# Stick-breaking attention: the second sigmoid is written over the scores in PSUM, and the scan reads it there

## The chip, the cores and the metric

One core of a Trainium2 chip runs the whole kernel in one launch. The metric is the device time in microseconds (us) of one execution, as the median of the runs made; every time below is in us or, for single instructions where it says so, in ns. The engines are PE (TensorE, matrix products and transposes), DVE (VectorE), ACT (ScalarE), POOL (GpSimd) and SP (SyncE, which here only issues transfers). PSUM is the memory into which PE writes, in eight banks of 512 fp32 values per partition; SBUF is the working memory.

## What is computed

The kernel is one inference step of a two-layer trunk: an attention layer with a compressed key-value latent, then a stick-breaking attention layer, each followed by a squared-ReLU network. The change touches the prompt part of the stick-breaking attention alone (1024 frames, 16 heads of 64):

```python
def sb_attend(q, q_pos, k, v, k_pos):
    z = jnp.einsum('bqhd,bkhd->bhqk', q, k, preferred_element_type=jnp.float32) * (SB_HEAD_DIM ** -0.5)
    mask = (k_pos[None, :] < q_pos[:, None])[None, None]
    log_keep = jnp.where(mask, jax.nn.log_sigmoid(-z), 0.0)
    suffix = lax.cumsum(log_keep, axis=3, reverse=True) - log_keep
    a = jnp.where(mask, jnp.exp(jax.nn.log_sigmoid(z) + suffix), 0.0)
    return jnp.einsum('bhqk,bkhd->bqhd', a.astype(v.dtype), v)
```

In products instead of logarithms: the weight of key k is sigmoid(z_k) times the product of sigmoid(-z_j) over all later keys j. The running product over the keys, from the last to the first, is a scan.

## The kernel before

`sb_attention_stage` handles two heads at a time, a pair; eight pairs make the stage. A pair is 16 steps. Step n is one head `a` and one block of 128 queries `q`, and has (q+1)*128 keys, its width `used`: 128 to 1024. The steps of a pair have, in order, the blocks q = 0, 1, 0, 1, 2, 3, 2, 3, 4, 5, 4, 5, 6, 7, 6, 7. Loops run over two pairs a body, `Fori` for three bodies and then a last one written out. The text counts the steps of a pair from 0 to 15.

One step passes through the engines like this:

- PE, `scores(i, n)` (L2015, L2019): q times the high and the low part of the keys into score buffer n % 2, and the causal mask added by one small product. A score buffer is two banks; there are two of them, banks 0 to 3.
- ACT, `weights(i, n)`: `keep` = sigmoid(-z) (L1850, tile e_u, two buffers in SBUF), then `take` = sigmoid(z) (L1854, tile e_b, four buffers in SBUF). Both read the scores in PSUM.
- DVE, `scan(i, n)` (L1956): the running product of `keep` from the last key to the first, into `rest` (e_r). Its second data operand is one zero per partition in SBUF, read for every element.
- POOL, `weigh(i, n)` (L1927): `take` times `rest`, in place in `take`; both in SBUF.
- PE, `transposes(i, n, last)` (L2040, for the next pair's queries and keys L2026): blocks of 128 keys, up to four to a task, into one of three task banks (4 to 6).
- ACT, `transposed_hi` (L1876; L1858 for queries and keys), copies a task bank rounded to the high part, and DVE, `transposed_lo` (L1980, L1962), writes the difference between the task bank and the high part.
- PE, `values(i, unit, last)` (L74 to L76), after every second step: weights times values into bank 7.

Each engine works its list in the order written out. In the body for n the lists are: PE scores(n+5), transposes(n+1), and for odd n values; ACT weights(n+5), transposed_hi(n+2); DVE scan(n+3), transposed_lo(n); POOL weigh(n+3). Semaphores tie the lists together. Those that matter here are `kept` (counts L1850), `taken` (L1854), `scanned` (L1956), `weighted` (L1927) and `t_lo`: scores(n) waits until take(n-2) is done, since both use one score buffer; keep(n) waits for scan(n-2), since both use one `keep` buffer; scan(n) waits for keep(n) and for weigh(n-2); the transposes of a task wait for the `lo` of three tasks earlier; scores of step 0 of a pair wait for its queries and keys.

Of the kernel before, what the change touches and what calls it, by code (L numbers as in the profile page):

```python
# [33 lines left out]
ACT = mybir.ActivationFunctionType  # L34
# [3 lines left out]
P = 128  # L38
D_MODEL = 1024
KT = D_MODEL // P  # L40
SEQ = 1024
# [1694 lines left out]
def sb_attention_stage(nc, io, scratch, raw):  # L1736
# [7 lines left out]
    with nc.cleanup_on_exit(), ExitStack() as ctx:  # L1744
        def sb(name, shape, dt=F32):
            return ctx.enter_context(nc.sbuf_tensor(name, shape, dt))
# [7 lines left out]
        v = [[sb(f"e_v{u}{s}", [P, NPT, 3 * SB_DIM], F32R) for s in "hl"] for u in range(2)]  # L1754
        raw_heads(nc, ctx, "e")
        v_raw = raw[2][:, :, :, 0, :]
        keep = [sb(f"e_u{u}", [P, SEQ]) for u in range(2)]
        take = [sb(f"e_b{u}", [P, SEQ]) for u in range(4)]
        rest = [sb(f"e_r{u}", [P, SEQ + 1]) for u in range(2)]
        pt = [[sb(f"e_pt{u}{s}", [P, NPT, GQ], F32R) for s in "hl"] for u in range(2)]  # L1760
# [6 lines left out]
        v_in, v_hi, v_lo = (signal(f"e_v_{x}") for x in ("in", "hi", "lo"))  # L1767
        arrived = [*raw_in, v_in]
        s_done = signal("e_s")
        kept, taken = signal("e_kept", 2), signal("e_taken", 2)  # L1770
        scanned, weighted = signal("e_scan", 2), signal("e_weighted", 2)
        t_done, t_hi, t_lo = signal("e_t"), signal("e_t_hi"), signal("e_t_lo", 3)
        pv_done, o_done = signal("e_pv", 2), signal("e_o", 1)
# [63 lines left out]

        @block.scalar
        def _(act):
            kept.start(act)  # L1840
            taken.start(act)
            o_done.start(act)

            def weights(i, n, last=False):

                first, _, used = score_columns(S.where(n)[2])
                z = score[n % 2][:, first:first + used]
                s_done.wait(act, S.STEPS * i + n + 1)
                scanned.wait(act, S.STEPS * i + n - 1)
                act.activation(keep[n % 2][:, 0:used], z, ACT.Sigmoid, scale=-SB_SCALE).then_inc(kept.sem, 1)  # L1850
                if n >= 4:

                    t_done.wait(act, S.PREPARE + TASKS * i + S.before(n - 3, last))
                act.activation(take[n % 4][:, 0:used], z, ACT.Sigmoid, scale=SB_SCALE).then_inc(taken.sem, 1)  # L1854

            def prepare_hi(pair, index, m):
                hi = operand(pair, index)[0]
                act.copy(hi, task_bank(m)[:, 0:hi.shape[1]]).then_inc(t_hi.sem, 1)  # L1858

            def values_hi(p, pair):  # L1860
                v_in.wait(act, 16 * (p + 1))
                pv_done.wait(act, S.UNITS // 2 * (p - 1))
                act.copy(v[pair][0][:].rearrange("p t (b c) -> p t b c", b=3)[:, :, ::2, :],
                         v_raw).then_inc(v_hi.sem, 1)

            def transposed_hi(i, n, last):
                unit, at = n // 2, (n % 2) * P
                for j, (kind, task) in enumerate(S.tasks(n, last)):
                    m = S.before(n, last) + j
                    t_done.wait(act, S.PREPARE + TASKS * i + m + 1)  # L1870
                    if kind == "prepare":
                        prepare_hi(1 - S.where(n)[0], task, m)
                        continue
                    pv_done.wait(act, S.UNITS * i + unit - 1)
                    s0 = task[0][1]
                    act.copy(pt[unit % 2][0][:, s0:s0 + len(task), at:at + P],  # L1876
                             task_bank(m)[:, 0:len(task) * P].rearrange("p (s c) -> p s c", c=P)).then_inc(
                                 t_hi.sem, 1)

            def output(i, g):  # L1880
                pv_done.wait(act, S.UNITS * i + 2 * g + 2)
                o_out[g % 2].wait(act, 16 * (S.GROUPS // 2 * i + g // 2))
                act.copy(o_st[g % 2][:], bank[:, 7, 0:GQ]).then_inc(o_done.sem, 1)

            def step(i, n, last):

                if not (last and n + S.AHEAD >= S.STEPS):
                    weights(i, n + S.AHEAD, last)
                pair, m = S.where(n)[0], n % S.PAIR_STEPS
                if m == S.VALUES_AT and not (last and pair == 1):  # L1890
                    values_hi(2 * i + pair + 1, 1 - pair)

            def body(i, last):
                for n in range(S.STEPS):
                    m = n + S.OUTPUT_LAG
                    if not (last and m >= S.STEPS):
                        step(i, m, last)
                    if n % 4 == 3:
                        output(i, n // 4)
                    if not (last and m >= S.STEPS):  # L1900
                        transposed_hi(i, m, last)

            for m in range(S.PREPARE):
                t_done.wait(act, m + 1)
                prepare_hi(0, m, m)
            v_in.wait(act, 16)
            const_done.wait(act, 4)
            act.copy(v[0][0][:].rearrange("p t (b c) -> p t b c", b=3)[:, :, ::2, :],
                     v_raw).then_inc(v_hi.sem, 1)
            for n in range(S.AHEAD):  # L1910
                weights(0, n)
            for n in range(S.OUTPUT_LAG):
                step(0, n, False)
                transposed_hi(0, n, False)
            bodies(act, body)
# [23 lines left out]
        @block.vector  # L1939
        def _(dve):  # L1940
            scanned.start(dve)
            t_lo.start(dve)
            for x in (*v[0], *v[1]):
                dve.memset(f32(x[:, :, SB_DIM:2 * SB_DIM]), 0.0).then_inc(const_done.sem, 1)
            for x in (*pt[0], *pt[1]):
                dve.memset(f32(x[:, 0, 0:P]), 0.0).then_inc(const_done.sem, 1)
            for x in rest:
                dve.memset(x[:, SEQ:SEQ + 1], 1.0).then_inc(const_done.sem, 1)
            dve.memset(zero[:], 0.0).then_inc(const_done.sem, 1)
            const_done.wait(dve, 11)  # L1950

            def scan(i, n):
                used = (S.where(n)[2] + 1) * P
                kept.wait(dve, S.STEPS * i + n + 1)
                weighted.wait(dve, S.STEPS * i + n - 1)
                dve.tensor_tensor_scan(rest[n % 2][:, SEQ - used:SEQ][:, ::-1], keep[n % 2][:, 0:used][:, ::-1],  # L1956
                                       zero[:].broadcast_to([P, used]), 1.0, ALU.mult, ALU.add).then_inc(
                                           scanned.sem, 1)

            def prepare_lo(pair, index, m):  # L1960
                hi, lo, rows = operand(pair, index)
                dve.tensor_tensor(lo, task_bank(m)[rows, 0:hi.shape[1]], f32(hi[rows, :]), ALU.subtract).then_inc(  # L1962
                    t_lo.sem, 1)

            def values_lo(p, pair):
                v_hi.wait(dve, p + 1)
                hi, lo = (x[:].rearrange("p t (b c) -> p t b c", b=3)[:, :, ::2, :] for x in v[pair])
                dve.tensor_tensor(lo, v_raw, f32(hi), ALU.subtract).then_inc(v_lo.sem, 1)

            def transposed_lo(i, n, last):  # L1970
                unit, at = n // 2, (n % 2) * P
                for j, (kind, task) in enumerate(S.tasks(n, last)):
                    m = S.before(n, last) + j
                    t_hi.wait(dve, S.PREPARE + TASKS * i + m + 1)
                    if kind == "prepare":
                        prepare_lo(1 - S.where(n)[0], task, m)
                        continue
                    s0 = task[0][1]
                    hi, lo = (x[:, s0:s0 + len(task), at:at + P] for x in pt[unit % 2])
                    dve.tensor_tensor(lo, task_bank(m)[:, 0:len(task) * P].rearrange(  # L1980
                        "p (s c) -> p s c", c=P), f32(hi), ALU.subtract).then_inc(t_lo.sem, 1)

            def body(i, last):
                for n in range(S.STEPS):
                    if not (last and n + S.AHEAD >= S.STEPS):
                        scan(i, n + S.AHEAD)
                    pair, m = S.where(n)[0], n % S.PAIR_STEPS
                    if m == S.VALUES_AT and not (last and pair == 1):
                        values_lo(2 * i + pair + 1, 1 - pair)
                    transposed_lo(i, n, last)  # L1990

            for m in range(S.PREPARE):
                t_hi.wait(dve, m + 1)
                prepare_lo(0, m, m)
            values_lo(0, 0)
            for n in range(S.AHEAD):
                scan(0, n)
            bodies(dve, body)

        @block.tensor  # L2000
        def _(pe):
# [3 lines left out]
            def scores(i, n):  # L2005
                pair, a, q = S.where(n)
                if n % S.PAIR_STEPS == 0:

                    last_task = S.before((n - S.PAIR_STEPS) + S.PREPARE_AT[-1] + 1) if n else 0
                    t_lo.wait(pe, S.PREPARE + TASKS * i + last_task)  # L2010
                taken.wait(pe, S.STEPS * i + n - 1)
                first, chunks, used = score_columns(q)
                for at, width, key in chunks:
                    for k in k_tt[pair]:
# [388 lines left out]
```

## Time and profile before

| what | value |
|---|---|
| median of 3 runs | 3258.3 us (3256.64 to 3260.61) |
| span of the profiled execution, first to last instruction | 3254.2 us |
| what lies around that span, against the median | 4.1 us |
| stick-breaking prompt stage, in that span | from 1793 to 2192.5 us, 399.5 us |
| one pair of heads in it, steady state | 48.8 us |

The profile is of one execution. A page of it gives the busy time of each engine over the span; the busy time of PE includes modelled ends of pipelined products. The windows view gives the same for any stretch, with the granted clock of TensorE as a share of full speed. The timeline gives start and duration of single instructions, with neighbours of one shape merged (x2 is two instructions, and the duration runs from the start of the first to the end of the last). Successive instructions of one engine overlap a little, so distances between starts are shorter than durations. No own time is listed for the profiled execution beside its span; sums are made on the span, and the 4.1 us around it are taken as unchanged.

### The profile page before, as it was taken

What the parts mean: (1) busy time and instruction counts of PE and PEld (TensorE: products, weight loads), DVE (VectorE), ACT (ScalarE), POOL (GpSimd) and SP (SyncE); (2) the same over time, 40 slices, a digit from 0 to 9 for tenths busy, and PEclk for the clock granted to TensorE, in tenths of its full rate; (3) what the DMA queues carried; (4) which work ended last, traced back from release to release, by engine and by line L of the source; (5) the groups of instructions that cost most, each with busy time, mean ns of one, the idle gap of its engine ahead of it and who ended that gap; (6) DMA issues with size and microseconds to landing.
All of it is one profiled execution on the core that took longest, in us unless ns stands there. A gap on an engine that the chain in (4) does not pass through costs nothing. (4 is left out here: it accounts for less than half of the span.)

```text
span 3254.2 us, 43271 instructions
## 1 busy us (share of the span) xinstructions
PE 3016.3 (93%) x16123; PEld 2670.9 (82%) x16123; DVE 1308.7 (40%) x1944; ACT 1000.7 (31%) x1923; POOL 591.0 (18%) x418
## 2 busy tenths in 40 slices
PE   7989987999999999998999788878799999999998
PEld 6778875889889998897887666767688988999987
DVE  5556652333223332242000889882233332333323
ACT  4344443231112221132111667662313211122112
POOL 3100001021112211121000344440103121122111
PEclk9999997999999999999999999996699999999999
DMA  4211114211011111102323332303302111111111
GB/s 142 75 41 41 43 35 156 83 52 46 26 39 52 52 45 32 39 27 81 101 94 88 74 69 56 70 11 125 136 1 59 45 32 38 39 52 52 41 37 72
DMA packets 224436, 194.72 MB, mean 60 GB/s; under 512 B 80976, under 2 KB 190032, under 8 KB 224336
## 3 DMA queue, kind: packets, MB, share of 16 engines
q1 hardware_dynamic: 224336, 193.37, 20.0%
q8 instruction: 65, 1.06, 0.1%
q14 instruction: 35, 0.29, 0.0%
HBM read 158.83 MB, written 34.50 MB: 59 GB/s over the span
## 5 line engine op out<-in xcount | busy, mean ns | idle before, releaser
L1449 DVE TENSOR_TENSOR x<-m_ps,x 128x512 f32<-128x512 f32 x324 | 224.0, 691 | 670.5 <-PE m_ps L76 670.5
L1484 DVE TENSOR_TENSOR m_sq<-m_relu 128x384 f32<-128x384 f32 x192 | 170.7, 889 | 524.4 <-ACT m_relu L1388 524.4
L74 PE MATMUL m_ps<-h_h,m_up0h 128*128 128x384 f32 x768 | 259.3, 338 | 8.2 <-POOL m_up0l L1422 8.2
L76 PE MATMUL m_ps<-h_h,m_up0l 128*128 128x384 f32 x768 | 258.8, 337 | 0.0
L75 PE MATMUL m_ps<-h_l,m_up0h 128*128 128x384 f32 x768 | 258.7, 337 | 0.0
L76 PE MATMUL m_ps<-h_h,m_up1l 128*128 128x384 f32 x768 | 256.9, 335 | 0.0
L74 PE MATMUL m_ps<-h_h,m_up1h 128*128 128x384 f32 x768 | 256.9, 335 | 0.0
L75 PE MATMUL m_ps<-h_l,m_up1h 128*128 128x384 f32 x768 | 256.9, 335 | 0.0
L1388 ACT ACTIVATE m_relu<-m_ps 128x384 f32<-128x384 f32 x192 | 94.5, 492 | 514.6 <-PE m_ps L76 514.6
L1956 DVE TENSOR_TENSOR_SCAN e_r<-e_u,e_zero 128x128 f32<-128x128 f32 (+7 forms) x128 | 217.9, 1702 | 2.4 <-ACT e_u L1850 0.7
L1927 POOL TENSOR_TENSOR e_b<-e_b,e_r 128x128 f32<-128x128 f32 (+7 forms) x128 | 162.6, 1271 | 289.1 <-DVE e_r L1956 268.3
L1383 ACT CAST m_dn0h<-m_dn_raw 128x1024 fp32r<-128x1024 f32 x16 | 16.8, 1051 | 547.6 <-PE m_ps L76 547.6
L74 PEld LDWEIGHTS m_ps<-h_h,m_up0h 128*128 128x128 f32 x768 | 145.7, 190 | 9.2 <-POOL m_up0l L1422 8.6
L75 PEld LDWEIGHTS m_ps<-h_l,m_up0h 128*128 128x128 f32 x768 | 145.7, 190 | 0.5
L76 PEld LDWEIGHTS m_ps<-h_h,m_up0l 128*128 128x128 f32 x768 | 145.5, 190 | 0.0
L74 PEld LDWEIGHTS m_ps<-h_h,m_up1h 128*128 128x128 f32 x768 | 144.3, 188 | 0.0
L75 PEld LDWEIGHTS m_ps<-h_l,m_up1h 128*128 128x128 f32 x768 | 144.3, 188 | 0.0
L76 PEld LDWEIGHTS m_ps<-h_h,m_up1l 128*128 128x128 f32 x768 | 144.2, 188 | 0.0
L1422 POOL TENSOR_TENSOR m_up0l<-m_up_raw,m_up0h 128x1024 fp32r<-128x1024 f32 x32 | 76.6, 2394 | 320.0 <-ACT m_up0h L1376 320.0
L1429 POOL TENSOR_TENSOR m_dn0l<-m_dn_raw,m_dn0h 128x1024 fp32r<-128x1024 f32 x16 | 38.5, 2409 | 528.8 <-ACT m_dn0h L1383 528.8
L2040 PE MATMUL e_ps<-ident,e_b 128*128 128x128 f32 x576 | 91.0, 280 | 36.9 <-DVE e_pt0l L1980 18.9
L1488 DVE TENSOR_TENSOR m_ul<-m_sq,m_uh 128x384 fp32r<-128x384 f32 x192 | 113.3, 590 | 19.1 <-DVE m_sq L1484 1.7
(465 smaller groups left out, 7674.6 us busy)
## 6 DMA issues: line engine op xcount, KB each, us to landing
m_up_raw<-in_mlp_w_up SPq DMA_DIRECT2D x64, 512.0 KB, 4.7
m_dn_raw<-in_mlp_w_down SPq DMA_DIRECT2D x64, 512.0 KB, 3.7
d_raw_q<-scratch_q SPq DMA_DIRECT2D x32, 256.0 KB, 4.3
d_raw_k<-new_p_sb_k SPq DMA_DIRECT2D x32, 256.0 KB, 5.1
h_raw<-scratch_oT SPq DMA_DIRECT2D x4, 1536.0 KB, 16.9
scratch_qr<-a_qrst SPq DMA_DIRECT2D x9, 512.0 KB, 3.4
scratch_q<-d_out SPq DMA_DIRECT2D x18, 256.0 KB, 2.0
a_x<-in_x_prompt SPq DMA_DIRECT2D x8, 512.0 KB, 4.9
```

What stands on the lines that cost most here:

```text
L74: pe.matmul(out, w[0], m[0], start=start, stop=False)
L75: pe.matmul(out, w[0], m[1], start=False, stop=False)
L76: return pe.matmul(out, w[1], m[0], start=False, stop=stop)
L1388: act.activation(relu[n % 2][:], bank[:, (n + 2) % 4, 0:GROUP], ACT.Relu).then_inc(relu_done.sem, 1)
L1422: pool.tensor_tensor(w_up[j % 2][1][:], up_raw[:], f32(w_up[j % 2][0][:]), ALU.subtract).then_inc(up_lo.sem, 1)
L1429: pool.tensor_tensor(w_dn[j][1][:], dn_raw[:], f32(w_dn[j][0][:]), ALU.subtract).then_inc(dn_lo.sem, 1)
L1449: dve.tensor_tensor(x[:, t, cols], bank[:, 4 + n % 3, :], x[:, t, cols], ALU.add).then_inc(added.sem, 1)
L1484: dve.tensor_tensor(sq[n % 2][:], relu[n % 2][:], relu[n % 2][:], ALU.mult).then_inc(sq_done.sem, 1)
L1488: dve.tensor_tensor(u_t[1][:, j, cols], sq[n % 2][:], f32(u_t[0][:, j, cols]), ALU.subtract).then_inc(u_lo.sem, 1)
L1927: pool.tensor_tensor(b, b, rest[n % 2][:, SEQ - used + 1:SEQ + 1], ALU.mult).then_inc(weighted.sem, 1)
L1956: dve.tensor_tensor_scan(rest[n % 2][:, SEQ - used:SEQ][:, ::-1], keep[n % 2][:, 0:used][:, ::-1], zero[:].broadcast_to([P, used]), 1.0, A ...
L2040: t = pe.transpose(task_bank(m)[:, c * P:(c + 1) * P], take[n % 4][:, k * P:(k + 1) * P], ident[:])
```

## The change

The `keep` buffers in SBUF go. ACT makes `take` first and `keep` second, and writes `keep` over the scores in PSUM. The scan reads `keep` there. The score buffer is free for the next scores only when the scan of it is done, so scores(n) waits for scan(n-2) where it waited for take(n-2). ACT no longer waits for `scanned`.

```diff
-        keep = [sb(f"e_u{u}", [P, SEQ]) for u in range(2)]
...
-        kept, taken = signal("e_kept", 2), signal("e_taken", 2)
+        kept, taken = signal("e_kept"), signal("e_taken")
...
-            kept.start(act)
-            taken.start(act)
             o_done.start(act)
...
                 s_done.wait(act, S.STEPS * i + n + 1)
-                scanned.wait(act, S.STEPS * i + n - 1)
-                act.activation(keep[n % 2][:, 0:used], z, ACT.Sigmoid, scale=-SB_SCALE).then_inc(kept.sem, 1)
                 if n >= 4:
 
                     t_done.wait(act, S.PREPARE + TASKS * i + S.before(n - 3, last))
                 act.activation(take[n % 4][:, 0:used], z, ACT.Sigmoid, scale=SB_SCALE).then_inc(taken.sem, 1)
+                act.activation(z, z, ACT.Sigmoid, scale=-SB_SCALE).then_inc(kept.sem, 1)
...
             def scan(i, n):
-                used = (S.where(n)[2] + 1) * P
+                first, _, used = score_columns(S.where(n)[2])
+                keep = score[n % 2][:, first:first + used]
                 kept.wait(dve, S.STEPS * i + n + 1)
                 weighted.wait(dve, S.STEPS * i + n - 1)
-                dve.tensor_tensor_scan(rest[n % 2][:, SEQ - used:SEQ][:, ::-1], keep[n % 2][:, 0:used][:, ::-1],
+                dve.tensor_tensor_scan(rest[n % 2][:, SEQ - used:SEQ][:, ::-1], keep[:, ::-1],
                                        zero[:].broadcast_to([P, used]), 1.0, ALU.mult, ALU.add).then_inc(
                                            scanned.sem, 1)
...
-                taken.wait(pe, S.STEPS * i + n - 1)
+                scanned.wait(pe, S.STEPS * i + n - 1)
```

## Rows read from the trace of the kernel before

**Rows 1.** Windows view of one pair: busy time per engine, instructions, granted clock.

```profile
core 0: us, PE busy (x) PEld busy (x) DVE busy (x) ACT busy (x) POOL busy (x), PEclk, DMA share, GB/s
1937.00:1985.80 48.80, 39.13 (x292) 33.09 (x290) 43.76 (x51) 34.40 (x70) 20.24 (x17) 1.00 0.32 64
```

**Rows 2.** Waits of DVE in this pair: total, times, longest.

```profile
DVE e_pt1l L1980 <- ACT e_pt1h L1876: 2.7, 1, 2.7
DVE e_pt0l L1980 <- ACT e_pt0h L1876: 1.8, 1, 1.8
```

**Rows 3.** Scan's source line, minimum/median/maximum ns, then groups by form.

```profile
L1956 DVE TENSOR_TENSOR_SCAN e_r<-e_u,e_zero x128: 406/1651/3262, 1803.2 to 2181.9; 128x128 f32<-128x128 f32 x16, 128x256 f32<-128x256 f32 x16, 128x384 f32<-128x384 f32 x16, 128x512 f32<-128x512 f32 x16
...
L1956 DVE TENSOR_TENSOR_SCAN e_r<-e_u,e_zero 128x384 f32<-128x384 f32 x16 | 15.3, 957 | 0.4
L1956 DVE TENSOR_TENSOR_SCAN e_r<-e_u,e_zero 128x1024 f32<-128x1024 f32 x16 | 48.3, 3016 | 0.0
L1956 DVE TENSOR_TENSOR_SCAN e_r<-e_u,e_zero 128x128 f32<-128x128 f32 (+7 forms) x128 | 217.9, 1702 | 2.4 <-ACT e_u L1850 0.7 <-POOL e_b L1927 0.7
```

**Rows 4.** Timeline of POOL: start, duration, instruction.

```profile
1943.78 2.00 POOL L1927 TENSOR_TENSOR e_b<-e_b,e_r 128x1024 f32<-128x1024 f32 x1 [2.22 <-DVE e_r L1956]
...
1984.60 2.00 POOL L1927 TENSOR_TENSOR e_b<-e_b,e_r 128x1024 f32<-128x1024 f32 x1 [2.22 <-DVE e_r L1956]
```

**Rows 5.** Timeline of DVE.

```profile
1944.67 1.39 DVE L1956 TENSOR_TENSOR_SCAN e_r<-e_u,e_zero 128x128 f32<-128x128 f32 x1
...
1981.69 2.83 DVE L1956 TENSOR_TENSOR_SCAN e_r<-e_u,e_zero 128x1024 f32<-128x1024 f32 x1
1984.44 0.86 DVE L1980 TENSOR_TENSOR e_pt1l<-e_ps,e_pt1h 128x512 fp32r<-128x512 f32 x2
1985.22 0.41 DVE L1962 TENSOR_TENSOR e_k0l<-e_ps,e_k0h 128x256 fp32r<-128x256 f32 x1
1985.55 2.93 DVE L1956 TENSOR_TENSOR_SCAN e_r<-e_u,e_zero 128x896 f32<-128x896 f32 x1
1988.40 0.99 DVE L1980 TENSOR_TENSOR e_pt1l<-e_ps,e_pt1h 128x512 fp32r<-128x512 f32 x2
1989.32 3.16 DVE L1956 TENSOR_TENSOR_SCAN e_r<-e_u,e_zero 128x1024 f32<-128x1024 f32 x1
```

**Rows 6.** The low parts by form (one operand in PSUM), and of the values (both in SBUF).

```profile
L1980 DVE TENSOR_TENSOR e_pt0l<-e_ps,e_pt0h x96: 264/602/692, 1806.6 to 2187.0; 128x512 fp32r<-128x512 f32 x48, 128x128 fp32r<-128x128 f32 x16, 128x256 fp32r<-128x256 f32 x16, 128x384 fp32r<-128x384 f32 x16
...
L1980 DVE TENSOR_TENSOR e_pt0l<-e_ps,e_pt0h 128x512 fp32r<-128x512 f32 x48 | 31.5, 668 | 0.5 <-ACT e_pt0h L1876 0.3
L1980 DVE TENSOR_TENSOR e_pt0l<-e_ps,e_pt0h 128x128 fp32r<-128x128 f32 x16 | 4.4, 273 | 0.1
L1968 DVE TENSOR_TENSOR e_v0l<-d_raw_v,e_v0h 128x1024 fp32r<-128x1024 f32 x4 | 4.8, 1202 | 0.5 <-ACT e_v0h L1908 0.5
```

**Rows 7.** Timeline of PE: scores of step 15 and of the next pair's step 0.

```profile
1984.21 0.39 PE L2015 MATMUL e_ps<-e_k1h,e_q 128*128 128x512 f32 x1
...
1985.21 0.82 PE L2040 MATMUL e_ps<-ident,e_b 128*128 128x128 f32 x6
1985.79 0.36 PE L2015 MATMUL e_ps<-e_k0h,e_q 128*128 128x256 f32 x1
```

**Rows 8.** Timeline of ACT behind them.

```profile
1985.85 0.86 ACT L1876 CAST e_pt1h<-e_ps 128x512 fp32r<-128x512 f32 x2 [1.34 <-PE e_ps L2040]
1986.60 1.04 ACT L1850 ACTIVATE e_u<-e_ps 128x1024 f32<-128x1024 f32 x1
1987.51 1.04 ACT L1854 ACTIVATE e_b<-e_ps 128x1024 f32<-128x1024 f32 x1
```

**Rows 9.** Groups by form of the second sigmoid; DMA issues on SP's queue.

```profile
L1854 ACT ACTIVATE e_b<-e_ps 128x128 f32<-128x128 f32 (+7 forms) x128 | 86.0, 672 | 0.0
...
1946.99 4.79 SPq L1733 DMA_DIRECT2D d_raw_k<-new_p_sb_k  x4
```

## Prediction

> **What bounds the kernel now.** I first read the page for where the stage stands in the whole, then the windows view of one pair in its steady state. A pair takes 48.8 us, and DVE is busy for 43.8 of them, PE for 39.1, ACT for 34.4, POOL for 20.2 [rows 1]. So DVE comes nearest to setting the pace, but it isn't saturated: it is idle for 5.0 us, and the view of waits puts 4.5 of these into two places where it waits for ACT's high parts [rows 2]. These lie at the narrow steps 2 to 5, where DVE and ACT stand behind PE, which works off the long product of the values of the widest steps.
>
> The groups by form then show something odd in the scan, which is 217.9 us of DVE's work in the stage. Its shortest instruction of width 128 takes 406 ns, yet the longest of all is 3262 ns. Width 384 takes 957 ns, so 128 more elements cost 0.276 us; by that line width 1024 should take 2.34 us, but its mean is 3.02 [rows 3]. The timelines say why. A scan of width 128 starts at 1944.67 and takes 1.39 us instead of 0.41 [rows 5]; POOL has been in its product since 1943.78 and leaves it at 1945.78 [rows 4], and the scan ends 0.28 us after that. The scan of step 14 starts at 1985.55, POOL's product of step 13 runs from 1984.60 to 1986.60, and the scan takes 2.93 us [rows 4, 5] where the line gives 2.06. A scan that meets a running POOL product thus stands still for nearly all the overlap. The low parts (L1980) run beside the same POOL products and never exceed 692 ns, with a width of 512 at 668 in the mean [rows 6]: the one at 1984.44 is not held up by the product that starts at 1984.60 [rows 4, 5]. What sets them apart from the scan is that one of their two inputs lies in PSUM.
>
> **The change part by part.**
>
> *The scan's input moves to PSUM: less work on DVE.* It gets the same placement of inputs as L1980, one in PSUM and one in SBUF (the zero). So I take it to run free of POOL. Per head unblocked scans would cost, by the line, 8 widths with 0.406 each and 0+1+...+7 = 28 steps of 0.276, that is 10.97 us. There are 16 of each width, so 175.5 us in the stage. Against 217.9 that saves 42.4 us, 5.3 per pair. If PSUM doesn't free it, the saving is zero.
>
> The Trainium skill has this as a rule: in "SBUF — State Buffer", § Who interferes with whom, a DVE instruction with two SBUF inputs contends with a GpSimd instruction that reads SBUF, one with at most one SBUF input does not. The trace agrees with both halves, with 2.93 us against 2.06 and with 692 ns at most.
>
> *What a PSUM input costs in itself.* No scan reads PSUM before. The nearest rows are products of DVE: from 273 ns at width 128 and 668 at 512 with an input in PSUM, width 1024 would take 1.19 us, and with both inputs in SBUF it takes 1.20 [rows 6]. I take no difference; the bounds are 0 and 0.1 us per scan. The second sigmoid's output in PSUM has no row either; I take its present 672 ns in the mean [rows 9], between nothing less and twice that (below).
>
> The Trainium skill speaks against the change here: "VectorE: DVE Perf Modes", § The TRN2 errata, gives VectorE 120 cycles of fixed cost from PSUM and 58 from SBUF at 0.96 GHz, so by an estimate from that page 128 scans would lose 8 us of work. The rows of the low parts show no such difference.
>
> *The buffers: a longer hold.* Scores(n) waited for take(n-2), and now wait for scan(n-2). Before, this would often have come late: scores(15) start at 1984.21 and scan(13) ends at 1984.52; the next pair's scores(0) start at 1985.79 and scan(14) ends at 1988.48 [rows 5, 7]. Put against each other in this way, twelve of a pair's sixteen scores start before that scan's end, by 13.7 us together. Most of it costs nothing: PE is idle for 9.7 us of a pair [rows 1], and the largest part of this comes right after the scores, in the transposes, which wait for low parts that DVE makes after the same scan. PE gets its scores done later and waits less behind them.
>
> What it costs shows on DVE: a scan may now find its `keep` late. That is a ring over two steps: scan(n-2), scores(n), transposes(n-4), their copies, take(n), keep(n), scan(n). The transposes and copies are in it because PE and ACT have them ahead of the sigmoids in their lists. For step 15: scores 1.00 us (1984.21 to 1985.21), transposes 0.82, then 0.57 until ACT takes the first sigmoid at 1986.60, and 1.95 for both (to 1988.55) [rows 7, 8]. Together 4.34, and 0.08 for each of two hand-overs (scan(13) ends 1984.52, POOL starts 1984.60 [rows 4, 5]): 4.50. Meanwhile DVE does the low parts of step 10 (1984.52 to 1985.55, 1.03), scan(14), 2.06 when unblocked, and the low parts of step 11 (1988.48 to 1989.32, 0.84) [rows 5]: 3.93. So DVE would wait 0.57 us for keep(15). With step 14 at its present 2.93 it would have been 4.80 and no wait: the faster scan is what exposes the ring. The same sum, with the durations of the other widths, gives a wait at steps 4, 5, 7, 11, 12 and 15, of 0.25 to 0.57, and none at the other ten. That makes 2.9 us per pair; the two waits for the high parts [rows 2] stay, as PE's products of values in front of them do. The bounds are 0 (PE and ACT run ahead wherever they can) and 0.5 at all sixteen steps, 8.0.
>
> *The order on ACT.* `take` comes first, so POOL's second input is early and the scan's comes one sigmoid later, up to 1.04 us [rows 8]. This is in the ring. ACT loses its wait for `scanned`, which PE's wait now implies. Queued behind the waiting scores on PE are transposes and values; those who wait for them are in the ring too. `keep` also stands behind the wait for the transposes of four steps before, but ACT has copied these already.
>
> *Transfers.* SP issues what it did. The next pair's keys are issued until 1951.78 [rows 9], and a pair that is 2.4 us shorter takes little from a lead of several us. POOL's products lose their own blocked time, worth nothing on the path, as POOL is busy for 20.2 of 48.8 us [rows 1]. TensorE's granted clock is at 1.00 in the pair shown, so at its 2.4 GHz level, and PE will be idle for less.
>
> **Sum.** Per pair 5.3 - 2.9 = 2.4 us gained, over eight pairs 19.2. The span of 3254.2 becomes 3235.0; with 4.1 around it, 3239.1 for a median of 3258.3.
>
> **The rivals.**
>
> *The hold costs nothing:* PE and ACT find room and only the 5.3 us stay, 42 in all, 3216. For it speaks that PE and ACT are far from full [rows 1]; against it that the ring of step 15 comes out 0.57 us above DVE's own work though it has no slack of its own in it. 6%.
>
> *The scan stays blocked* (the zero in SBUF is read for every element, as now): no gain, and the ring shows only where scans are not blocked now, at the narrow steps 4, 5 and 7, for 1.2 us, of which PE regains about half before the widest steps. 0.7 per pair, 3264. Against it: the high part that L1980 reads in SBUF does it no harm. 10%.
>
> *Slower: the sigmoid written over its own input.* ACT would read and write one bank in the same instruction, and no row shows that. If it ran at half speed, each ring would grow by 0.67 us on average [rows 9]. At the six steps that already wait this makes 4.0 per pair, and if others join up to 5.4; less the 2.4, 1.6 to 3.0 per pair or 13 to 24 us, in the middle 3277. It decides from about 0.35 us more per step in the ring, wherever that comes from (six steps of 0.4 are 2.4). 10%.
>
> *The change does what I forecast:* 74%.
>
> **How the numbers follow.** The likeliest gives 3239. Its own range has 1.2 us per pair more or less on the waits and 0.1 us per scan on a PSUM input: 3228 to 3250. For 8 in 10 I go to 3222 on the side of the free hold and to 3264 on the side of a blocked scan; about 6% lie below and 13% above. This kernel's three runs tell a change from none at about 0.2%, 6.5 us. Faster by more than that: the forecast nearly whole and the free hold, 0.78. Within: part of the blocked scan and the forecast's tail, 0.09. Slower: the sigmoid and the rest of the blocked scan, 0.13.
>
> **What the profile after would show.** Scans of width 1024 at 2.3 to 2.4 us and of width 128 at 0.41, all alike within a width, 175 us in sum, whatever POOL does beside them. A pair of 46.4 us with DVE busy for 38.5. New waits of DVE for the second sigmoid of about half a microsecond, and of PE's scores for the scan. The second sigmoid still 1.04 us at width 1024. I am wrong if the widths still scatter (blocked), if the second sigmoid takes longer than the first, or if the waits of DVE for it come to 5 us per pair.

## The result

The changed kernel takes 3234.45 us in the median of four runs (3232.4 to 3237.93) against 3259.45 of the kernel before (four runs, 3256.64 to 3262.72). The medians lie 25 us apart; the ratio on record is 0.9933, with a 95% interval of 0.9915 to 0.9951: 0.7% faster, 22 us by the ratio. The forecast was 3239.1, 19 us less. The profiled execution has a span of 3235.9 us and a time of 3237.93, so 2.0 us lie around it. Of 3254.2 to 3235.9 the span lost 18.3.

The windows view of a pair of heads in steady state, to be held against [rows 1]:

```profile
core 0: us, PE busy (x) PEld busy (x) DVE busy (x) ACT busy (x) POOL busy (x), PEclk, DMA share, GB/s
1980.30:2026.60 46.30, 38.72 (x291) 33.16 (x290) 38.73 (x51) 34.35 (x71) 20.17 (x16) 1.00 0.34 68
```

A pair is 46.3 us long where it was 48.8, and DVE is busy in it for 38.7 where it was 43.8. ACT and POOL do the same work; POOL's 20.2 us are those of before, so its products had no blocked time of their own to lose. DVE has lost 5.0 us of work and the pair only 2.5, so DVE's idle time has grown from 5.0 to 7.6.

The scans by form, and the sigmoids (L1849 is `take`, L1850 `keep`, now with its output in PSUM), for [rows 3] and [rows 9]:

```profile
L1953 DVE TENSOR_TENSOR_SCAN e_r<-e_ps,e_zero 128x1024 f32<-128x1024 f32 x16 | 36.7, 2291 | 7.6 <-ACT e_ps L1850 7.6
L1953 DVE TENSOR_TENSOR_SCAN e_r<-e_ps,e_zero 128x384 f32<-128x384 f32 x16 | 15.3, 956 | 0.8
L1953 DVE TENSOR_TENSOR_SCAN e_r<-e_ps,e_zero 128x128 f32<-128x128 f32 x16 | 6.6, 415 | 1.2 <-ACT e_ps L1850 1.2
...
L1953 DVE TENSOR_TENSOR_SCAN e_r<-e_ps,e_zero 128x128 f32<-128x128 f32 (+7 forms) x128 | 173.2, 1353 | 23.7 <-ACT e_ps L1850 22.5
...
L1850 ACT ACTIVATE e_ps<-e_ps 128x128 f32<-128x128 f32 (+7 forms) x128 | 86.3, 674 | 0.0
```

The scan of width 1024 went from 3016 to 2291 ns in the mean, that of width 128 from 860 to 415; all of them from 217.9 to 173.2 us. Behind the bar is the new entry: DVE sat idle for 22.5 us before scans, waiting for `keep`. The sigmoid over its own input costs 674 ns in the mean, as one into SBUF did.

What one scan meets now, on the timelines of POOL and DVE:

```profile
1975.20 2.01 POOL L1923 TENSOR_TENSOR e_b<-e_b,e_r 128x1024 f32<-128x1024 f32 x1 [1.93 <-DVE e_r L1953]
```

```profile
1972.83 2.29 DVE L1953 TENSOR_TENSOR_SCAN e_r<-e_ps,e_zero 128x1024 f32<-128x1024 f32 x1 [0.17 <-ACT e_ps L1850]
1975.04 0.86 DVE L1977 TENSOR_TENSOR e_pt1l<-e_ps,e_pt1h 128x512 fp32r<-128x512 f32 x2
1975.82 0.41 DVE L1959 TENSOR_TENSOR e_k0l<-e_ps,e_k0h 128x256 fp32r<-128x256 f32 x1
1976.15 2.01 DVE L1953 TENSOR_TENSOR_SCAN e_r<-e_ps,e_zero 128x896 f32<-128x896 f32 x1
1978.08 1.00 DVE L1977 TENSOR_TENSOR e_pt1l<-e_ps,e_pt1h 128x512 fp32r<-128x512 f32 x2
1979.73 2.29 DVE L1953 TENSOR_TENSOR_SCAN e_r<-e_ps,e_zero 128x1024 f32<-128x1024 f32 x1 [0.65 <-ACT e_ps L1850]
```

These are steps 13 to 15 of a pair. The scan of step 14 starts while POOL is in the product of step 13, which runs to 1977.21, and takes 2.01 us; in the same place before it took 2.93 [rows 5]. Then DVE is idle for 0.65 us ahead of the scan of step 15. What that scan waited for, on PE and ACT:

```profile
1975.35 0.39 PE L2012 MATMUL e_ps<-e_k1h,e_q 128*128 128x512 f32 x1
...
1976.34 0.82 PE L2037 MATMUL e_ps<-ident,e_b 128*128 128x128 f32 x6
```

```profile
1976.99 0.86 ACT L1872 CAST e_pt1h<-e_ps 128x512 fp32r<-128x512 f32 x2 [1.22 <-PE e_ps L2037]
1977.73 1.04 ACT L1849 ACTIVATE e_b<-e_ps 128x1024 f32<-128x1024 f32 x1
1978.65 1.04 ACT L1850 ACTIVATE e_ps<-e_ps 128x1024 f32<-128x1024 f32 x1
```

Scan(13) ends at 1975.12, scores(15) start at 1975.35, transposes(11) at 1976.34, `take` at 1977.73, `keep` ends at 1979.69 and scan(15) starts at 1979.73: 4.61 us around.

### The profile page after: what moved, and what is told of

It reads as the page before. It is cut to its first block and busy times, and to the rows that moved or that the text cites. A ratio compares the mean times of both kernels' runs of the same rounds, so it can differ in the third digit from the quotient of the medians.

```text
span 3235.9 us, 43262 instructions
## 1 busy us (share of the span) xinstructions
PE 3014.2 (93%) x16123; PEld 2668.5 (82%) x16123; DVE 1266.5 (39%) x1944; ACT 1001.3 (31%) x1923; POOL 589.7 (18%) x418
## 3 DMA queue, kind: packets, MB, share of 16 engines
q1 hardware_dynamic: 224336, 193.37, 20.2%
## 5 line engine op out<-in xcount | busy, mean ns | idle before, releaser
L1953 DVE TENSOR_TENSOR_SCAN e_r<-e_ps,e_zero 128x128 f32<-128x128 f32 (+7 forms) x128 | 173.2, 1353 | 23.7 <-ACT e_ps L1850 22.5
L1422 POOL TENSOR_TENSOR m_up1l<-m_up_raw,m_up1h 128x1024 fp32r<-128x1024 f32 x32 | 76.7, 2398 | 209.6 <-ACT m_up1h L1376 209.6
```

Of the source, the lines that this page charges most:

```text
L1422: pool.tensor_tensor(w_up[j % 2][1][:], up_raw[:], f32(w_up[j % 2][0][:]), ALU.subtract).then_inc(up_lo.sem, 1)
```

## The experiments

Besides times and ratios to the kernel before, I give the length of a pair, as the distance from the mask product of step 0 (L2016 or L2019, with "causal_mask" in its row) to that of the next pair, and the sum of the 128 scans. The pair is the finer measure. It is the common value of the pairs after the first. In seven of the traces (before, e1, e2, e4, e7, e9, e10) the third pair is 0.5 to 1.5 us longer than its neighbours, and it is left out. In those of before, e2 and e7 PE waits there for a late transfer of the next pair's queries, for 1.26, 1.56 and 2.14 us. This is the row of the kernel before:

```profile
1904.05 0.66 PE L2026 MATMUL e_ps<-ident,d_raw_q 128*128 128x128 f32 x4 [1.26 <-DMA d_raw_q<-scratch_q]
```

It isn't a matter of the edit: e7 and e12 are one kernel, and only the trace of e7 has the long pair. In e5 and e6 the pairs differ more, so their range is given. Sums of scans and of waits are over the whole stage. The first and the last pair have larger waits than those between, so a wait of a steady pair isn't an eighth of the sum.

| kernel | median us | ratio (95%) | pair us | scans us | DVE waits for `keep` in the stage, us |
|---|---|---|---|---|---|
| before | 3253.84 to 3259.45 | 1 | 48.8 | 217.9 | 0.7 |
| changed | 3234.45 | 0.9933 (0.9915 to 0.9951) | 46.3 | 173.2 | 22.5 |
| e1, hold alone | 3255.21 | 0.9998 (0.9987 to 1.0008) | 48.9 | 215.2 | 1.0 |
| e2, before, thin product | 3213.09 | 0.9867 (0.9847 to 0.9887) | 43.85 | 172.9 | 1.1 |
| e3, changed, thin product | 3235.08 | 0.9933 (0.9914 to 0.9952) | 46.3 | 173.1 | 22.6 |
| e4, order alone | 3255.51 | 1.0004 (0.9994 to 1.0013) | 49.1 | 217.2 | 4.4 |
| e5, before, third sigmoid | 3262.02 | 1.0018 (1.0008 to 1.0027) | 48.7 to 52.0 | 218.1 | 4.7 |
| e6, changed, third sigmoid | 3274.23 | 1.0061 (1.0044 to 1.0078) | 50.4 to 53.7 | 173.5 | 66.8 |
| e7, changed, difference | 3215.32 | 0.9877 (0.986 to 0.9894) | 44.05 | 172.8 | 1.6 |
| e8, before, difference | 3254.76 | 0.9996 (0.9986 to 1.0007) | 48.4 to 48.8 | 215.7 | 0.4 |
| e9, thin product, hold | 3218.8 | 0.9889 (0.987 to 0.9909) | 44.6 | 173.2 | 1.7 |
| e10, thin product, order | 3222.1 | 0.9897 (0.9872 to 0.9922) | 45.1 | 173.1 | 13.4 |
| e11, changed, again | 3237.29 | 0.9946 (0.9925 to 0.9967) | 46.3 | 173.1 | 22.9 |
| e12, e7 again | 3216.98 | 0.9884 (0.9863 to 0.9905) | 44.1 | 172.8 | 1.6 |

### e1: the longer hold alone

```diff
                 taken.wait(pe, S.STEPS * i + n - 1)
+                scanned.wait(pe, S.STEPS * i + n - 1)
                 first, chunks, used = score_columns(q)
```

> The kernel before with one edit: scores(n) wait for scan(n-2) as well as for take(n-2). keep stays in SBUF and before take, the scans stay blocked by POOL's products. My theory (a ring through the scan, exposed only where scans aren't blocked): a pair of 49.2 to 50.0 us instead of 48.8, so 3 to 10 us slower in all, scans still 218 us in sum. Rival, the hold is passed on in full wherever scores now start before the scan's end (13.7 us a pair): 55 us a pair or more, over 50 us slower. Rival, the hold is free: 48.8, no change.

Measured: no change, 0.9998. The pair is 48.8 to 49.1 us, so 0.1 us longer in the middle of these and below the 49.2 that I had expected at least; the interval allows at most 2.6 us more in all. That is nearest to the rival by which the hold is free. The view of waits shows that the hold does bind. First the transposes of PE in the kernel before, then e1, both over the stage:

```profile
PE e_ps L2040 <- DVE e_pt0l L1980: 18.9, 20, 1.7
PE e_ps L2040 <- DVE e_pt1l L1980: 17.9, 8, 2.3
PE e_ps L2026 <- DVE e_pt0l L1980: 16.2, 15, 1.3
PE e_ps L2026 <- DVE e_pt1l L1980: 8.6, 12, 1.0
```

```profile
PE e_ps L2016 <- DVE e_r L1956: 64.3, 57, 2.1
PE e_ps L2027 <- DVE e_pt1l L1980: 2.5, 5, 0.5
```

PE waits for the scan 57 times and 64.3 us in sum, and gets nearly all of it back: in the kernel before its transposes waited 61.6 us for the low parts, which DVE makes behind the same scans, and about 5 are left of that here. A wait of an engine was moved, and the end didn't move.

### e2 and e3: POOL's product cut to one column

```diff
-                pool.tensor_tensor(b, b, rest[n % 2][:, SEQ - used + 1:SEQ + 1], ALU.mult).then_inc(
+                pool.tensor_tensor(b[:, 0:1], b[:, 0:1], rest[n % 2][:, SEQ - used + 1:SEQ - used + 2], ALU.mult).then_inc(
```

In the kernel before:

> The kernel before, with POOL's product of only one column of each step in place of all (the weights of the other columns are left as plain sigmoids). keep stays in SBUF and the hold is short. If POOL's product is what lengthens the scan: every scan on the line 0.41 us + 0.276 per 128 more, 175 us in sum instead of 218, a pair of 43.5 to 44.5 us and 35 to 42 us less in all. Rival, the scan in SBUF is slow for another reason (its placement, ACT's writes): scans stay at 218 us in sum, no change beyond 0.2%.

In the changed kernel:

> The changed kernel with the same one-column product on POOL. If the scan from PSUM no longer meets POOL, taking the product away changes nothing in the scans (173 us in sum as with the full product), and the pair stays within 0.5 us of 46.3; the time within 5 us of the changed kernel's 3234. Together with the run before it this says whether the change's whole gain is the block by POOL, less the ring. Rival, part of the block is left: scans shorter, 5 us or more gained.

These two kernels leave out the product of the other columns, and so do e9 and e10.

Measured: as the theory has it, on both sides. With the scan's input still in SBUF, taking POOL's product away brings the scans to 172.9 us and the pair to 43.85; with the input in PSUM it changes nothing. The groups by form, first of e2, then of e3:

```profile
L1956 DVE TENSOR_TENSOR_SCAN e_r<-e_u,e_zero 128x1024 f32<-128x1024 f32 x16 | 36.5, 2283 | 0.0
```

```profile
L1953 DVE TENSOR_TENSOR_SCAN e_r<-e_ps,e_zero 128x1024 f32<-128x1024 f32 x16 | 36.6, 2291 | 7.7 <-ACT e_ps L1850 7.7
```

2283 ns from SBUF without POOL, 2291 from PSUM with or without it. So the block by POOL was the whole of the scan's excess, and the move to PSUM removes all of it. The pair of 43.85 us puts the worth of removing the block at 4.95 us; and the changed kernel lies 2.45 us above it. This 2.45 is the price of the change. One reservation: the thin product also brings POOL's results earlier to the transposes. In the changed kernel that is worth nothing (e3, 46.3 us with both); for the kernel before no run separates it.

### e4: the order of the sigmoids alone

```diff
-                scanned.wait(act, S.STEPS * i + n - 1)
-                act.activation(keep[n % 2][:, 0:used], z, ACT.Sigmoid, scale=-SB_SCALE).then_inc(kept.sem, 1)
                 if n >= 4:
...
                 act.activation(take[n % 4][:, 0:used], z, ACT.Sigmoid, scale=SB_SCALE).then_inc(taken.sem, 1)
+                scanned.wait(act, S.STEPS * i + n - 1)
+                act.activation(keep[n % 2][:, 0:used], z, ACT.Sigmoid, scale=-SB_SCALE).then_inc(kept.sem, 1)
...
-                taken.wait(pe, S.STEPS * i + n - 1)
+                kept.wait(pe, S.STEPS * i + n - 1)
```

> The kernel before with take made first and keep second, keep still in SBUF; scores wait for keep(n-2), the last reader. Theory: ACT is more than a step ahead of DVE in the wide steps, so a keep that is one sigmoid later costs nothing there: within 0.2% of before, a pair of 48.8 to 49.1. Rival, the order is itself a cost that the change paid: waits of DVE for keep of 0.3 us or more at several steps, a pair of 50 us or more.

Measured: 1.0004, within its interval no change; a pair of 49.1 us, 0.3 more. While the scans are blocked, the order costs almost as little as the hold.

### e5 and e6: a third sigmoid

```diff
+                extra.wait(act, S.STEPS * i + n)
+                act.activation(junk[:, 0:used], z, ACT.Sigmoid, scale=SB_SCALE).then_inc(extra.sem, 1)
                 act.activation(take[n % 4][:, 0:used], z, ACT.Sigmoid, scale=SB_SCALE).then_inc(taken.sem, 1)
```

In the kernel before:

> The kernel before with a third sigmoid a step, of the same width, between keep and take, into a tile that nobody reads (0.58 us a step in ACT's list in the mean). ACT's busy time goes from 34.4 to about 43.5 us of a pair. No ring runs through the sigmoids and the scan here, and ACT stays under the pair's 48.8: 0 to 1.5 us more a pair, 0 to 12 in all.

In the changed kernel:

> The changed kernel with a third sigmoid a step, of the same width, before take and keep, into a tile that nobody reads. If the ring scan(n-2), scores(n), transposes(n-4), copies, sigmoids, scan(n) sets the pace, each step that already waits pays the whole 0.58 us: 3.5 to 5 us more a pair (46.3 to 50 or 51), 28 to 40 us more than the changed kernel's 3234, against 0 to 12 for the same edit in the kernel before. Rival, DVE's own work sets the pace in both and ACT has room: under 12 us in both.

Measured: the kernel before loses 0.2%, 6 us; the changed one goes to 3274.23, 40 us above its 3234.45 of other runs, or 37 above e11. In both traces two pairs are some 3 us longer than the others, and in each of these ACT is idle for 2.1 to 2.3 us before the first sigmoid of one step, with nothing in the profile that it waited for. This makes up most of the 6 us of e5; what it comes from is open. The pairs without it are 48.7 to 49.1 us in e5, where they were 48.8, and 50.4 to 51.9 in e6, where they were 46.3. The waits of DVE say it directly, first of e5, then of e6:

```profile
DVE e_r L1961 <- ACT e_u L1853: 4.7, 4, 2.1
```

```profile
DVE e_r L1958 <- ACT e_ps L1855: 66.8, 72, 3.2
```

The same 0.6 us a step are hidden in the one kernel and paid in the other, there by about half (40 us of 74 over the 128 steps), since DVE doesn't wait at every step. In the changed kernel the path of `keep` sets DVE's pace at the steps at which DVE waits.

### e7 and e8: the weight as a difference

`rest` at k is `keep` at k times `rest` at k+1, so `take` times `rest` is the difference of two neighbours of `rest`. ACT no longer makes `take`.

```diff
-                act.activation(take[n % 4][:, 0:used], z, ACT.Sigmoid, scale=SB_SCALE).then_inc(taken.sem, 1)
...
-                taken.wait(pool, S.STEPS * i + n + 1)
-                b = take[n % 4][:, 0:used]
-                pool.tensor_tensor(b, b, rest[n % 2][:, SEQ - used + 1:SEQ + 1], ALU.mult).then_inc(
+                if n >= 3:
+                    t_done.wait(pool, S.PREPARE + TASKS * i + S.before(n - 3, last))
+                r = rest[n % 2]
+                pool.tensor_tensor(take[n % 4][:, 0:used], r[:, SEQ - used + 1:SEQ + 1], r[:, SEQ - used:SEQ],
+                                   ALU.subtract).then_inc(
```

On the changed kernel:

> The changed kernel without take on ACT: since rest[k] = keep[k] * rest[k+1], the weight take[k] * rest[k+1] is rest[k+1] - rest[k], and POOL makes it with one subtraction of rest's neighbours. ACT loses 86 us of work and the ring loses one sigmoid (0.58 us a step in the mean, 0.85 at width 1024). Theory: all of the 2.8 us a pair for which DVE waits for keep goes, a pair of 43.5 to 44.3 us, 16 to 22 us less than the changed kernel's 3234: about 3215. Rival, those waits come from PE and not from the ring's length: 46 us a pair, within 5 us of 3234.

On the kernel before (scores wait for `keep`, their only reader now):

> The kernel before with the same subtraction on POOL, keep in SBUF. ACT loses the same 86 us of work, but the scans stay blocked by POOL (218 us in sum) and no ring runs through them, so little is gained: a pair of 48 to 48.8, 0 to 6 us less than before. If it gains as much as the run before it did over the changed kernel, ACT's work and not the ring was what mattered.

Measured: 3215.32 and a pair of 44.05 us on the changed kernel; nothing on the kernel before. The pair of e7 in the windows view and the waits of its DVE:

```profile
core 0: us, PE busy (x) PEld busy (x) DVE busy (x) ACT busy (x) POOL busy (x), PEclk, DMA share, GB/s
1980.00:2024.00 44.00, 38.26 (x290) 33.05 (x289) 38.49 (x51) 25.83 (x55) 19.12 (x17) 1.00 0.35 71
```

```profile
DVE e_pt1l L1975 <- ACT e_pt1h L1868: 22.4, 10, 3.1
...
DVE e_r L1951 <- ACT e_ps L1846: 1.6, 4, 0.7
```

The 22.5 us of waits for `keep` are 1.6, none of them in a steady pair, and a pair is 2.25 us shorter. ACT gave up 8.5 us of work a pair in e7 and about 7.5 in e8: it is no use where the scans are blocked, and worth 2.25 us a pair where they aren't. This version beats both kernels, by 1.2% and 0.6%.

### e9 and e10: what the 2.45 us are made of

Hold (the edit of e1) and order (the edits of e4), each with the one-column product, so without a block of the scans.

> The kernel before with the one-column product (no block of the scans) and the longer hold (scores also wait for scan(n-2)); keep in SBUF and still made first. It splits the 2.5 us a pair by which the changed kernel (46.3) stands above the kernel before with the thin product (43.85). If the ring is what counts, it has one sigmoid less here than in the changed kernel: for step 15 it is 4.50 - 0.91 = 3.59 us against 3.93 us of DVE's own work, so no wait: a pair of 43.9 to 44.4, the time within 5 us of 3213. If the hold is the price by itself: a pair of 46 or more, 3232.

> The kernel before with the one-column product and the order take, keep; keep in SBUF, scores wait only for keep(n-2). The other half of the split. No ring runs through the scan, so if the ring is what counts: a pair of 43.9 to 44.5, the time within 5 us of 3213, and the 2.5 us come only when hold and order meet. If the late keep is the price by itself: a pair of 46 or more, 3232.

Measured, against the pair of 43.85 in e2: the hold alone gives 44.6, so 0.8 more, and the order alone 45.1, so 1.25 more. Both are above what I expected, and their times lie 5.7 and 9.0 us above e2's 3213.1 where I had said within 5. The intervals of these times overlap with that of e2; the lengths of the pairs are what tells them apart. Waits of DVE for `keep`, first of e9, then of e10:

```profile
DVE e_r L1956 <- ACT e_u L1850: 1.7, 4, 0.7
```

```profile
DVE e_r L1956 <- ACT e_u L1854: 13.4, 32, 0.7
```

So the price isn't one that arises only where hold and order meet. Of the 2.45 us about half is the order, a third the hold, and 0.4 their meeting. Both are nearly free on top of blocked scans (0.3 and 0.1) and both cost once the scans are short.

They do it in different ways. In a steady pair of e10 DVE waits for `keep` at steps 5, 11 and 15, for 0.29, 0.41 and 0.68 us (and in some pairs for 0.17 at step 4), much as in the changed kernel. In a steady pair of e9 it doesn't wait for `keep` at all, and the four waits of its row lie in the first and the last pair; its 0.8 us are 0.4 more of waiting for high parts and 0.3 more of busy time of DVE, though its scans take the same. Only with hold and order together are there waits at steps 7, 12 and 13 too, 0.84 us in sum.

Step 15 shows how the order works. These are rows of e2's timeline (`keep` first, short hold, no block), of DVE and of ACT:

```profile
2006.24 2.28 DVE L1956 TENSOR_TENSOR_SCAN e_r<-e_u,e_zero 128x1024 f32<-128x1024 f32 x1
...
2012.39 2.28 DVE L1956 TENSOR_TENSOR_SCAN e_r<-e_u,e_zero 128x1024 f32<-128x1024 f32 x1
```

```profile
2011.16 1.04 ACT L1850 ACTIVATE e_u<-e_ps 128x1024 f32<-128x1024 f32 x1
2012.08 1.04 ACT L1854 ACTIVATE e_b<-e_ps 128x1024 f32<-128x1024 f32 x1
```

And its scores of that step on PE:

```profile
2008.78 0.39 PE L2015 MATMUL e_ps<-e_k0h,e_q 128*128 128x512 f32 x1
```

Scan(13) ends at 2008.52 and the scores start at 2008.78, 0.26 later, though they don't wait for it; in the changed kernel they start 0.23 later, with no idle time of PE before them. PE's own list, with the values of two steps ahead of them, brings them there in both. But the place of that list is itself set by DVE. These are the last waits of PE before scores(15), first in the changed kernel, before scores(14), then in e2 and e10, before the transposes of step 10, with the scores(15) of e10 last:

```profile
1971.47 0.50 PE L2012 MATMUL e_ps<-e_k1h,e_q 128*128 128x512 f32 x1 [1.26 <-DVE e_r L1953]
```

```profile
2005.71 0.77 PE L2040 MATMUL e_ps<-ident,e_b 128*128 128x128 f32 x5 [0.72 <-DVE e_pt0l L1980]
```

```profile
1964.00 0.77 PE L2040 MATMUL e_ps<-ident,e_b 128*128 128x128 f32 x5 [1.18 <-DVE e_pt0l L1980]
...
1967.06 0.39 PE L2015 MATMUL e_ps<-e_k1h,e_q 128*128 128x512 f32 x1
```

In the changed kernel PE waits for scan(12) by the hold; in e2 and e10 it waits for the low parts that DVE makes right after scan(12). Scores(15) start 3.94 us after the end of scan(12) in the changed kernel, 3.70 in e2 and 3.69 in e10. So PE is tied to DVE with the hold and without it, and here the hold adds 0.24 us at most.

The last waits of PE in e10 before the scores of steps 5 and 11, the other two at which DVE waits there, are of the same kind:

```profile
1981.82 0.65 PE L2026 MATMUL e_ps<-ident,d_raw_q 128*128 128x128 f32 x4 [0.50 <-DVE e_pt1l L1980]
...
1997.73 0.65 PE L2026 MATMUL e_ps<-ident,d_raw_k 128*128 128x128 f32 x4 [1.32 <-DVE e_pt0l L1980]
```

Behind the scores of step 15, e2 and the changed kernel differ. In e2 `keep` is ready at 2012.20, 3.68 us after scan(13), and DVE comes for it after 3.87. In the changed kernel it is ready after 4.57. The 0.9 us between them is `take`, which goes first. The wait for scan(13) does nothing at this step, and e10, which doesn't have it, waits for `keep`(15) just as long (0.68 us against 0.65).

### e11 and e12: the changed kernel and the difference, again

> The changed kernel again, on the chip and against the runs of the kernel before that the others of this call have: 0.9933 again, within its interval of 0.9915 to 0.9951.

> The subtraction on POOL with keep in PSUM, again, beside the changed kernel in one call: a pair of 44.05 us, and 0.5 to 0.7% less time than the changed kernel; a ratio of 0.986 to 0.989 to the kernel before.

Measured: 0.9946 for the changed kernel, within the interval named, and 0.9884 for the difference, whose 3216.98 is 0.6% below the 3237.29 beside it.

## Why the prediction was right, step by step

**The block.** That POOL's product holds up the scan, that it would end with one input in PSUM, and its size of 5.3 us a pair all came out: 44.7 us less in the scans (42.4 forecast, since the line from widths 128 and 384 was a little too steep: 175.5 us against 173), 5.0 of DVE's work a pair. e2 and e3 show the cause, from both sides: no product or no second SBUF input, the scans are the same 173 us. So the rival with a scan that stays blocked is out. The "SBUF — State Buffer" page of the Trainium skill, § Who interferes with whom, has the rule that fits: a DVE instruction with two SBUF inputs contends with a GpSimd instruction that reads SBUF. The runs agree with it, 217.9 us against 173. The pair gained 4.95 in e2, nearly all of the 5.3. That POOL's products would lose blocked time of their own was wrong, though it was given no price: they take 20.2 us a pair before and after.

**A PSUM input's own cost.** I took none. 2291 ns from PSUM against 2283 from SBUF without block is 8 ns. The 65 ns that follow, as an estimate, from the 120 and 58 cycles in "VectorE: DVE Perf Modes" of the Trainium skill, § The TRN2 errata, don't show; the measurement decides.

**The waits for `keep`.** Forecast 2.9 us a pair at six steps. A steady pair has 2.4: 0.30, 0.30, 0.59, 0.37, 0.17 and 0.65 us at steps 5, 7, 11, 12, 13 and 15; I had 4, 5, 7, 11, 12 and 15. The 22.5 us of the stage would be 2.8 a pair, but they hold larger waits in the first and the last pair. The round of step 15 was summed to 4.50 us and is 4.61, DVE's own work beside it to 3.93 and is 3.96 (4.61 less the wait of 0.65), so the wait of 0.57 is 0.65.

**The size was right, its reason only in part.** I called it a ring through the hold: scan(n-2) must end before scores(n). For step 15, the one that I worked out, it was luck that the sum came out: scan(13) doesn't hold up scores(15). PE's list puts them there, its place is set by DVE one step earlier, with the hold or without it, and what the change adds is the sigmoid `take` ahead of `keep`. I had put the order's cost "in the ring", and e10 shows that it stands without the hold: 1.25 us a pair. The hold itself is worth 0.8 (e9). That the faster scan exposes the waits, where the blocked one hid them, is shown: the same two edits cost 0.1 and 0.3 on blocked scans (e1, e4) and 0.8 and 1.25 on free ones (e9, e10). What closes the loop when there is no hold can be read from e10's trace: at each of the steps 5, 11 and 15, at which DVE waits, the last wait of PE before the scores is for low parts, 0.50, 1.32 and 1.2 us long. The prediction had these waits of PE as something that the hold would only replace. That they are what ties the two engines without the hold is a reading of rows; no run took them away.

**The sum.** 5.3 - 2.9 = 2.4 a pair stands against 4.95 - 2.45 = 2.5 measured; both terms are about 0.4 smaller than forecast, and the two errors cancel, which is luck too. In all, 19 us were forecast; the profiled spans give 18.3, of which 0.65 is the long pair that only the trace of before has; the first ratio gives 22 and that of e11 18. The two intervals together (0.9915 to 0.9967) leave 11 to 28 us open.

**The rivals.** The free hold (3216) fell: e2 and e7 are what it would have looked like. The slow sigmoid over its own input fell with 674 ns against 672. What I had not weighed as a rival is the order, since I had put it inside the ring.

## What to carry to other kernels

When one instruction's duration scatters at a fixed shape, lay the timeline of the other engines beside it before costing anything: here some 44 us of DVE's busy time were a standstill behind GpSimd, and moving one of two inputs to PSUM removed it. A block that is taken away uncovers what it hid, so cost a late input or a longer hold against the new durations, not the old; on the old ones it may measure as nothing, as e1 and e4 did. And once the scan is short, look at what its producer does first: dropping an operation ahead of it (e7) was worth as much again as the change.

## What the runs showed of the hardware

A scan whose first input lies in SBUF, and whose second is one value per partition in SBUF, is held up by a GpSimd product that reads SBUF: 2.93 us at width 896 against 2.01 in the same place with the first input in PSUM, and 3016 ns against 2291 in the mean at width 1024. With the first input in PSUM the second in SBUF does no harm. Whether the single value counts as an input where the first is in SBUF is not shown, since no run left it out of SBUF. The product isn't lengthened in turn (2.00 us at width 1024 before, 2.01 after). A sigmoid that writes over its own input in PSUM runs at the speed of one into SBUF, 1050 and 1049 ns at width 1024. A scan reads PSUM as fast as SBUF, 2291 and 2283 ns at width 1024.
